# Feed-forward steps on TensorE: both high-part products in a row, then both low-part products

## The chip, the cores and the metric

The kernel runs on one core of a Trainium2 chip. The metric is the device time of one execution in microseconds (us); less is better. Its outputs are float32, and the products are made from float32 numbers split in two parts (below).

## What is computed

One layer of a small hybrid network on 256 tokens of width 1024. A mixing block (a gated linear recurrence beside an attention) is followed by a feed-forward block, and the change lies in the latter alone. Cut to that block:

```
hf = rms_norm(x, ffn_norm_g)
up = causal_depthwise_conv(hf @ w_up, ffn_conv_w, ffn_conv_b)   # w_up: 1024 x 5632, 3 taps
gate, val = split(up, 2)                                        # 2816 channels each
x = x + (gelu(gate) * val) @ w_down                             # w_down: 2816 x 1024
```

## The kernel before

**Units.** All weights come as a stream of units of 128 x 1024 float32 numbers, two to a DMA. ScalarE copies a unit to `w_hi` in the type fp32r (line L381), VectorE puts what that leaves out into `w_lo` (L703). Both tiles are rings of six buffers. The activations are split in the same way, into `h_hi` and `h_lo`, which lie side by side in `h_both`. A product is the sum of high x high, high x low and low x high.

**Steps.** The 2816 channels are 22 steps of 128 channels, numbered s = 0 to 21. A step has three units: gate, value and down. `ffn_up(s)` makes the gate's and the value's products. For each of the two, eight matmuls with 512 columns (L1419, "high" below) multiply `w_hi` with `h_hi` and `h_lo` at once, into the two halves of a bank, and then eight with 256 columns (L1423, "low") add `w_lo` times `h_hi` to the first half. The last of the low ones raises `unit_used`. `ffn_down(s)` has twelve matmuls of 512 columns (L1062, L1063, L1066), in the order high-high, low weights, low activations.

**What follows an up unit.** When `unit_used` says that a gate or value is complete, ScalarE copies the second half of its bank (`cross`, L614), and VectorE adds the first half to it (`join`, L985). ScalarE then makes the first tap of the convolution (`base`, L622), VectorE the other two (`taps`, L992 and L996), ScalarE the GELU (L628), VectorE the product with the value (`prod`, L1005), ScalarE its high part (`act_hi`, L634) and VectorE its low part (`act_lo`, L1010). Only `act_lo` raises `act_ready`, for which `ffn_down` waits.

**The order on the engines** is written out by hand, and each engine runs in order. TensorE takes `ffn_up(t)`, then `ffn_down(t - 2)`. ScalarE and VectorE, in their step t, split the weights for up(t) and down(t-2), and between these they evict what up(t-1) left:

```
# ScalarE, step t                     # VectorE, step t
hi(down_unit(t - LAG)); hi(g)         lo(down_unit(t - LAG)); lo(g)
ffn_cross(t - 1, 0)                   ffn_join(t - 1, 0)
hi(v)                                 lo(v)
ffn_cross(t - 1, 1)                   ffn_join(t - 1, 1)
ffn_base(t - 1, 0)                    ffn_taps(t - 1, 0)
ffn_act_hi(t - 2)                     ffn_act_lo(t - 2)
ffn_base(t - 1, 1)                    ffn_taps(t - 1, 1)
ffn_gelu(t - 1)                       ffn_prod(t - 1)
```

Steps 0 and 1 have code of their own on TensorE (L1372 for the high, L1383 for the low products, all of 256 columns). Steps 2 to 21 use `ffn_up`, 20 in all. The end has no up unit left to hide behind. After up(21) and down(19) TensorE goes to `ffn_end`: it waits for `act_ready` of step 20, makes three pieces of down(20), waits for `act_hi_done` of step 21, makes three pieces of down(21) (each waits for `act_ready` of step 21 before its third matmul), and then the remaining pieces of 256 columns. Beside it ScalarE and VectorE run one last step in the order above, without a gate unit: there the down unit of step 21 (`U_LAST`) stands where v stood, between the two crosses and the two joins. Up banks alternate: banks 0 and 1 in even steps, 6 and 7 in odd ones, the gate in the first of each pair.

Of the kernel before, what the change touches and what calls it, by code (L numbers as in the profile page):

```python
# [52 lines left out]
RING = 6  # L53
# [26 lines left out]
def up_units(s):  # L80
    at = U_FFN + max(3 * s - 1, 0)
    return at, at + 1
# [26 lines left out]
def build_layer(nc, x, stream, params, gates, out):  # L109
    with ExitStack() as ctx:  # L110
        def sb(name, shape, dt=F32):
            return ctx.enter_context(nc.sbuf_tensor(name, shape, dt))
# [7 lines left out]
        w_hi = [sb(f"w_hi{r}", [P, UNIT], F32R) for r in range(RING)]  # L120
        w_lo = [sb(f"w_lo{r}", [P, UNIT], F32R) for r in range(RING)]
# [120 lines left out]
        def by_chunk(tile):  # L242

            return tile[:, :].rearrange("p (kc n) -> p kc n", kc=KC)

        def up_bank(s, which):

            return bank[(0, 1, 6, 7)[2 * (s % 2) + which]]
# [21 lines left out]
        def hi_count(u):  # L270

            return u + 1 - sum(v <= u for v in VECTOR_HI)

        def lo_count(u):

            return LO_UNITS.index(u) + 1 if u in LO_UNITS else u + 1
# [24 lines left out]
        def at_pass(it, per, value):  # L301

            return value if it is None else it * per + value
# [755 lines left out]
        def _(pe):  # L1059
# [8 lines left out]
            def split(u, it=None):  # L1068

                pe.wait_ge(lo_done, at_pass(it, LOOP_UNITS, lo_count(u)))  # L1070
# [250 lines left out]
            for j in range(LC):  # L1321
                if j == LC - 1:
                    out_sums()
                u = U_O + j
# [87 lines left out]
            def ffn_up(s, it=None):  # L1412
                for which, u in enumerate(up_units(s)):
                    if s >= 2:
                        pe.wait_ge((joined_g, joined_v)[which], at_pass(it, LOOP_STEPS, s - 1))
                    whi, wlo, acc = by_chunk(w_hi[u % RING]), by_chunk(w_lo[u % RING]), up_bank(s, which)
                    pe.wait_ge(hi_done, at_pass(it, LOOP_UNITS, hi_count(u)))
                    for kc in range(KC):
                        pe.matmul(acc[:, :], whi[:, kc, :], h_both[:, kc, :, :].rearrange("p b t -> p (b t)"),  # L1419
                                  start=kc == 0, stop=False)  # L1420
                    split(u, it)
                    for kc in range(KC):
                        ins = pe.matmul(acc[:, 0:SEQ], wlo[:, kc, :], h_hi[:, kc, :], start=False, stop=kc == KC - 1)  # L1423
                    ins.then_inc(unit_used, 1)
# [34 lines left out]
            for t in range(LAG, PEELED):  # L1459
                ffn_up(t)  # L1460
                ffn_down(t - LAG)
            with pe.Fori(0, PASSES - 1) as it:
                for t in range(PEELED, PEELED + LOOP_STEPS):
                    ffn_up(t, it)
                    ffn_down(t - LAG, it)
# [64 lines left out]
```

## Time and profile before

| | |
|---|---|
| median of 3 runs | 290.15 us (289.98 to 290.15) |
| the profiled execution, its own time | 290.13 us |
| its span in the trace | 288.4 us, so 1.7 us lie outside it |
| TensorE (PE) busy | 284.1 us, 99% of the span |
| VectorE (DVE) busy | 244.2 us, 85% |
| ScalarE (ACT) busy | 202.9 us, 70% |
| feed-forward steps in `ffn_up` | 20, from about 113.8 us on |

The end of a matmul is modelled in the trace, and matmuls are pipelined, so busy shares of TensorE say little. What counts is how far apart they start, or the pieces of the chain of work that ended last, which run from one end to the next. A "weight load" (PEld) is the instruction ahead of each matmul that brings its stationary operand.

### The profile page before, as it was taken

How to read it: one execution, taken by the hardware profiler on the slowest of the kernel's cores; microseconds unless marked ns; L12 is line 12 of the kernel's file. 1: busy time of each engine (PE TensorE's matmuls, PEld its weight loads, DVE VectorE, ACT ScalarE, POOL GpSimd, SP SyncE). 2: the span in 40 equal slices, each digit the busy share in tenths (PEclk: the TensorE clock that was granted, in tenths of full speed). 3: DMA queues.
4: the chain of work that ended last, by engine and by line, in shares of the span. 5: the costliest groups of instructions: out<-in, count | busy, mean ns of one | idle time of the engine just before them, and what ended most of it. 6: DMA issues, size and time to landing. Idle time of an engine off the chain costs nothing.

```text
span 288.4 us, 5012 instructions
## 1 busy us (share of the span) xinstructions
PE 284.1 (99%) x1642; PEld 246.6 (86%) x1642; DVE 244.2 (85%) x448; ACT 202.9 (70%) x389; POOL 11.4 (4%) x26
## 2 busy tenths in 40 slices
PE   8999999999999999999999999999999999999996
PEld 7688999898788999888888888888888888888885
DVE  2998898889999888999988788888888888888765
ACT  4893599999897687778676766667666666676540
POOL 3000004600000000000000000000000000000000
PEclk9999999999999999999999999999999999999999
DMA  7999950440365705375647474544647454100003
GB/s 276 428 419 419 398 186 7 148 145 14 134 228 209 257 38 164 130 291 166 278 145 287 148 261 177 160 162 152 252 145 291 145 181 178 77 0 0 0 0 145
DMA packets 8111, 52.23 MB, mean 181 GB/s; under 512 B 928, under 2 KB 1312, under 8 KB 2080
## 3 DMA queue, kind: packets, MB, share of 16 engines
q1 hardware_dynamic: 7920, 51.50, 48.1%
q0 software_dynamic: 176, 0.53, 0.5%
q8 instruction: 9, 0.15, 0.2%
q14 instruction: 6, 0.05, 0.0%
HBM read 50.98 MB, written 1.05 MB: 180 GB/s over the span
## 4 chain that ended last, share of the span: by engine, by line
PE 95%; DMA 2%; DVE 1%; ACT 1%; SPq 0%; issue 0%
PE bank L1419 25%; PE bank L1062 15%; PE bank L1063 14%; PE bank L1066 14%; PE bank L1423 13%; PE bank L1118 3%; PE bank L1372 3%; DMA x_tok<-in_x_dram 2%; PE bank L1383 1%; PE bank L1182 1%; PE bank L1306 1%; PE bank L1213 1%; PE bank L1222 1%; PE bank L1339 1%; PE bank L1176 1%; DVE w_hi L691 0%
## 5 line engine op out<-in xcount | busy, mean ns | idle before, releaser
L703 DVE TENSOR_TENSOR w_lo<-raw,w_hi 128x1024 fp32r<-128x1024 f32 x93 | 110.9, 1221 | 4.5 <-ACT w_hi L381 3.9
L381 ACT ACTIVATE w_hi<-raw 128x1024 fp32r<-128x1024 f32 x83 | 84.2, 1058 | 2.3 <-PE bank L1066 1.9
L1419 PE MATMUL bank<-h_both,w_hi 128*128 128x512 f32 x320 | 79.6, 391 | 0.0
L1419 PEld LDWEIGHTS bank<-h_both,w_hi 128*128 128x128 f32 x320 | 58.8, 188 | 11.3
L1423 PEld LDWEIGHTS bank<-h_both,w_lo 128*128 128x128 f32 x320 | 43.7, 191 | 3.1
L1423 PE MATMUL bank<-h_both,w_lo 128*128 128x256 f32 x320 | 44.7, 283 | 0.0
L614 ACT ACTIVATE tanh_a<-bank 128x256 f32<-128x256 f32 x44 | 16.7, 381 | 38.7 <-PE bank L1423 38.7
L1063 PE MATMUL bank<-w_lo,act_hi 128*128 128x512 f32 (+1 forms) x90 | 34.9, 388 | 0.0
L1062 PE MATMUL bank<-w_hi,act_hi 128*128 128x512 f32 (+1 forms) x90 | 34.9, 388 | 0.0
L1066 PE MATMUL bank<-w_hi,act_lo 128*128 128x512 f32 (+1 forms) x90 | 34.6, 385 | 0.0
L622 ACT ACTIVATE xc<-ygate,par 128x256 f32<-128x256 f32 x44 | 26.2, 596 | 4.2 <-DVE ygate L985 4.2
L985 DVE TENSOR_TENSOR ygate<-bank,tanh_a 128x256 f32<-128x256 f32 x44 | 18.6, 422 | 12.1 <-ACT tanh_a L614 12.0
L996 DVE SCALAR_TENSOR_TENSOR xc<-ygate,par,xc 128x254 f32<-128x254 f32 x44 | 21.3, 483 | 5.1 <-DVE xc L992 0.2
L992 DVE SCALAR_TENSOR_TENSOR xc<-ygate,par,xc 128x255 f32<-128x255 f32 x44 | 21.2, 481 | 3.2 <-ACT xc L622 3.2
L1066 PEld LDWEIGHTS bank<-w_hi,act_lo 128*128 128x128 f32 x90 | 16.9, 188 | 3.5
L1062 PEld LDWEIGHTS bank<-w_hi,act_hi 128*128 128x128 f32 x90 | 17.0, 189 | 2.9
L1063 PEld LDWEIGHTS bank<-w_lo,act_hi 128*128 128x128 f32 x90 | 17.0, 189 | 2.6
L1062 PE MATMUL bank<-h_both,w_hi 128*128 128x256 f32 x64 | 18.6, 291 | 0.0
L1063 PE MATMUL bank<-h_both,w_hi 128*128 128x256 f32 x64 | 18.1, 283 | 0.0
L1066 PE MATMUL bank<-h_both,w_lo 128*128 128x256 f32 x64 | 18.1, 283 | 0.0
L628 ACT ACTIVATE gate_r<-xc 128x256 f32<-128x256 f32 x22 | 9.2, 418 | 11.1 <-DVE xc L996 11.1
L1062 PE MATMUL bank<-w_hi,mix_hi 128*128 128x512 f32 (+1 forms) x36 | 13.5, 374 | 0.0
(193 smaller groups left out, 411.4 us busy)
## 6 DMA issues: line engine op xcount, KB each, us to landing
raw<-in_stream_dram SPq DMA_DIRECT2D x47, 1024.0 KB, 4.8
x_tok<-in_x_dram SPq DMA_DIRECT2D x2, 512.0 KB, 5.0
out_dram<-x_tok SPq DMA_DIRECT2D x3, 256.0 KB, 2.1
p_T<-in_gates_dram POOLq DMA_DIRECT2D x1, 512.0 KB, 9.5
out_dram<-x_tok SPq DMA_DIRECT2D x2, 128.0 KB, 2.0
par<-in_params_dram SPq DMA_DIRECT2D x1, 117.0 KB, 6.6
mix_g<-in_params_dram POOLq DMA_DIRECT2D x1, 4.0 KB, 5.6
```

What stands on the lines that cost most here:

```text
L381: act.activation(hi_tile(u)[:, :], raw_unit(u), ACT.Copy).then_inc(hi_done, 1)
L614: act.activation(cross[which][s % 2], up_bank(s, which)[:, SEQ:2 * SEQ], ACT.Copy).then_inc(cross_out, 1)
L622: act.activation((conv_g, conv_v)[which][s % 2], joined[which][s % 2], ACT.Identity, bias=par[:, bass.ds(col + FFN_B, 1)], scale=par[:, ba ...
L703: dve.tensor_tensor(w_lo[u % RING][:, :], raw_unit(u), hi_tile(u)[:, :].bitcast(F32), ALU.subtract).then_inc(lo_done, 1)
L985: dve.tensor_tensor(joined[which][s % 2], up_bank(s, which)[:, 0:SEQ], cross[which][s % 2], ALU.add).then_inc((joined_g, joined_v)[which], 1)
L992: dve.scalar_tensor_tensor(acc[:, 1:SEQ], joined[which][s % 2][:, 0:SEQ - 1], par[:, bass.ds(col + (FFN_W + 2 * STEPS), 1)], acc[:, 1:SEQ] ...
L996: dve.scalar_tensor_tensor(acc[:, 2:SEQ], joined[which][s % 2][:, 0:SEQ - 2], par[:, bass.ds(col + FFN_W, 1)], acc[:, 2:SEQ], ALU.mult, AL ...
L1062: pe.matmul(acc, lhs_hi, rhs_hi, start=first, stop=False, skip_group_check=resumed)
L1063: pe.matmul(acc, lhs_hi, rhs_lo, start=False, stop=False, skip_group_check=resumed)
L1066: return pe.matmul(acc, lhs_lo, rhs_hi, start=False, stop=last, skip_group_check=resumed)
L1419: pe.matmul(acc[:, :], whi[:, kc, :], h_both[:, kc, :, :].rearrange("p b t -> p (b t)"), start=kc == 0, stop=False)
L1423: ins = pe.matmul(acc[:, 0:SEQ], wlo[:, kc, :], h_hi[:, kc, :], start=False, stop=kc == KC - 1)
```

## The change

In `ffn_up` the loop over gate and value is cut in two. The first loop makes the high products of the gate and then those of the value; the second makes the low products of the gate and then those of the value. The down unit follows as before. The number of matmuls, their shapes and their operands stay, and so do the waits, each of which goes with the products that it guards. The other engines' programs are the same.

```diff
                 for which, u in enumerate(up_units(s)):
                     if s >= 2:
                         pe.wait_ge((joined_g, joined_v)[which], at_pass(it, LOOP_STEPS, s - 1))
-                    whi, wlo, acc = by_chunk(w_hi[u % RING]), by_chunk(w_lo[u % RING]), up_bank(s, which)
+                    whi, acc = by_chunk(w_hi[u % RING]), up_bank(s, which)
                     pe.wait_ge(hi_done, at_pass(it, LOOP_UNITS, hi_count(u)))
                     for kc in range(KC):
                         pe.matmul(acc[:, :], whi[:, kc, :], h_both[:, kc, :, :].rearrange("p b t -> p (b t)"),
                                   start=kc == 0, stop=False)
+                for which, u in enumerate(up_units(s)):
+                    wlo, acc = by_chunk(w_lo[u % RING]), up_bank(s, which)
                     split(u, it)
                     for kc in range(KC):
                         ins = pe.matmul(acc[:, 0:SEQ], wlo[:, kc, :], h_hi[:, kc, :], start=False, stop=kc == KC - 1)
                     ins.then_inc(unit_used, 1)
```

TensorE's rows in the last step of the loop's body, before the change, with the semaphores that a row waits for; bank6 is the gate's and bank7 the value's:

```order
L1066 MATMUL bank3<-w_hi2,act_lo 128x512
L1415 REGISTER_ALU
L1419 MATMUL bank6<-h_both,w_hi0 128x512 [waits hi_done,joined_g]
L1419 MATMUL bank6<-h_both,w_hi0 128x512 x7
L1070 REGISTER_ALU
L1423 MATMUL bank6<-h_both,w_lo0 128x256 [waits lo_done]
L1423 MATMUL bank6<-h_both,w_lo0 128x256 x7
L1419 MATMUL bank7<-h_both,w_hi1 128x512 [waits hi_done,joined_v]
L1419 MATMUL bank7<-h_both,w_hi1 128x512 x7
L1070 REGISTER_ALU
L1423 MATMUL bank7<-h_both,w_lo1 128x256 [waits lo_done]
L1423 MATMUL bank7<-h_both,w_lo1 128x256 x7
```

The same place in the changed kernel:

```order
L1419 MATMUL bank6<-h_both,w_hi0 128x512 [waits hi_done,joined_g]
L1419 MATMUL bank6<-h_both,w_hi0 128x512 x7
L1419 MATMUL bank7<-h_both,w_hi1 128x512 [waits hi_done,joined_v]
L1419 MATMUL bank7<-h_both,w_hi1 128x512 x7
L1070 REGISTER_ALU
L1425 MATMUL bank6<-h_both,w_lo0 128x256 [waits lo_done]
L1425 MATMUL bank6<-h_both,w_lo0 128x256 x7
L1070 REGISTER_ALU
L1425 MATMUL bank7<-h_both,w_lo1 128x256 [waits lo_done]
L1425 MATMUL bank7<-h_both,w_lo1 128x256 x7
L1070 REGISTER_ALU
L1062 MATMUL bank4<-w_hi5,act_hi 128x512 [waits act_ready,lo_done]
```

The gate's low products have moved behind the value's high ones, so that wide matmuls stand next to wide ones and narrow next to narrow, and the gate (bank6) is complete eight wide matmuls later than before, while the value (bank7) keeps its place in the count.

After the last step the rows of TensorE are the same in both kernels; these are the first of `ffn_end` (bank4 holds a piece of the output):

```order
L1062 MATMUL bank4<-w_hi2,act_hi 128x512 [waits act_ready,lo_done]
L1063 MATMUL bank4<-w_lo2,act_hi 128x512
L1066 MATMUL bank4<-w_hi2,act_lo 128x512
```

## Rows read from the trace of the kernel before

**Rows 1.** The page: busy time, and the chain that ended last by engine.
```profile
PE 284.1 (99%) x1642; PEld 246.6 (86%) x1642; DVE 244.2 (85%) x448; ACT 202.9 (70%) x389; POOL 11.4 (4%) x26
...
PE 95%; DMA 2%; DVE 1%; ACT 1%; SPq 0%; issue 0%
```

**Rows 2.** Busy time by stretch, of one step: PE, PEld, DVE, ACT, POOL, clock.
```profile
180.26:188.57 8.31, 8.31 (x46) 7.17 (x44) 6.92 (x12) 5.50 (x10) 0.00 (x0) 1.00 0.54 170
```

**Rows 3.** The chain in order of time: start us, us, what; steps 10 and 21.
```profile
180.43 1.81 PE bank L1419 x8
182.24 0.95 PE bank L1423 x8
183.19 1.84 PE bank L1419 x8
185.03 0.95 PE bank L1423 x8
...
271.80 1.81 PE bank L1419 x8
```

**Rows 4.** The chain in order of time, steps 0 to 2.
```profile
108.19 1.92 PE bank L1383 x16
...
113.94 1.84 PE bank L1419 x8
```

**Rows 5.** Timeline, steps 2 and 3: start us, us, engine, line, instruction.
```profile
118.53 0.42 DVE L1010 TENSOR_TENSOR act_lo<-gate_i,act_hi 128x256 fp32r<-128x256 f32 x1
119.37 0.40 PE L1062 MATMUL bank<-w_hi,act_hi 128*128 128x512 f32 x1
121.13 1.05 ACT L381 ACTIVATE w_hi<-raw 128x1024 fp32r<-128x1024 f32 x1
122.11 0.62 PE L1419 MATMUL bank<-h_both,w_hi 128*128 128x512 f32 x2
122.91 1.22 DVE L703 TENSOR_TENSOR w_lo<-raw,w_hi 128x1024 fp32r<-128x1024 f32 x1
124.05 0.42 DVE L985 TENSOR_TENSOR ygate<-bank,tanh_a 128x256 f32<-128x256 f32 x1
124.38 0.48 DVE L992 SCALAR_TENSOR_TENSOR xc<-ygate,par,xc 128x255 f32<-128x255 f32 x1
```

**Rows 6.** Timeline, step 21 and the end.
```profile
274.60 0.38 ACT L614 ACTIVATE tanh_a<-bank 128x256 f32<-128x256 f32 x1 [1.65 <-PE bank L1423]
274.88 1.05 ACT L381 ACTIVATE w_hi<-raw 128x1024 fp32r<-128x1024 f32 x1
...
275.97 1.22 DVE L703 TENSOR_TENSOR w_lo<-raw,w_hi 128x1024 fp32r<-128x1024 f32 x1 [0.52 <-ACT w_hi L381]
...
277.81 0.42 DVE L985 TENSOR_TENSOR ygate<-bank,tanh_a 128x256 f32<-128x256 f32 x1 [0.62 <-ACT tanh_a L614]
...
278.30 0.48 DVE L992 SCALAR_TENSOR_TENSOR xc<-ygate,par,xc 128x255 f32<-128x255 f32 x1
...
279.22 0.42 DVE L1010 TENSOR_TENSOR act_lo<-gate_i,act_hi 128x256 fp32r<-128x256 f32 x1
...
279.76 0.19 PEld L1062 LDWEIGHTS bank<-w_hi,act_hi 128*128 128x128 f32 x1
279.95 0.39 PE L1062 MATMUL bank<-w_hi,act_hi 128*128 128x512 f32 x1
...
281.12 0.42 ACT L634 ACTIVATE act_hi<-gate_i 128x256 fp32r<-128x256 f32 x1 [1.36 <-DVE gate_i L1005]
...
281.57 0.43 DVE L1010 TENSOR_TENSOR act_lo<-gate_i,act_hi 128x256 fp32r<-128x256 f32 x1 [0.49 <-ACT act_hi L634]
...
282.46 0.39 PE L1066 MATMUL bank<-w_hi,act_lo 128*128 128x512 f32 x1
```

**Rows 7.** Timeline, where TensorE had waited for VectorE.
```profile
12.09 0.18 PEld L1118 LDWEIGHTS bank<-w_hi,h_both 128*128 128x128 f32 x1 [0.32 <-DVE w_hi L691]
12.12 0.47 PE L1118 MATMUL bank<-w_hi,h_both 128*128 128x512 f32 x1
```

## The prediction, made before the changed kernel ran

> **What bounds the kernel now.** I read the page first. TensorE is busy for 99% of the span, and of the chain that ended last 95% is TensorE [rows 1]. The reader should not stop at the busy share, since ends of matmuls are modelled; so the second view is one step of the feed-forward block by stretch. It takes 8.31 us, TensorE fills it at the full granted clock (1.00, that is 2.4 GHz), VectorE is busy for 6.92 us of it and ScalarE for 5.50 [rows 2]. The third view is the chain in order of time. From step 10 to step 21 the gate's high products begin at 180.43 and 271.80 [rows 3]: 11 steps in 91.37 us, 8.31 each, without a piece of another engine between. In the steady steps nothing is waited for on TensorE, so only its own spacing can give time back there. The last view is the timeline of the end, where up products no longer cover what follows them: there the other engines can take time away.
>
> **Part 1: spacing on TensorE, 20 steps.** Inside a step the two groups of eight high matmuls do the same work, yet the gate's takes 1.81 us and the value's 1.84 [rows 3]. The gate's follows a down unit (512 columns), the value's follows low products (256 columns). So a group of wide matmuls behind narrow ones costs 0.03 us more. It does not grow with the number of narrow ones ahead: the first high group of step 2 comes behind 5.75 us of 256-column matmuls (108.19 to 113.94, some 48 at 0.12 each) and takes 1.84 as well [rows 4]. In the changed kernel the value's high group follows the gate's high group, so I give it 1.81: 0.03 us less a step. The down unit still follows narrow products and pays as before. Against this, eight low ones behind wide ones take 0.95 us [rows 3], and 16 in a row 1.92, so 0.96 for a second eight [rows 4]; the 16 low ones of a step will take 0.95 + 0.96 instead of 2 x 0.95, 0.01 more. Net 0.02 us a step, and over 20 steps 0.4 us saved. Its bounds: 0 if the 0.03 us belong to something else than the neighbour, 20 x 0.03 = 0.6 if the second low group costs nothing more.
>
> **Part 2: the waits in the steady steps.** The value's high products now start where the gate's low ones did, 0.95 us sooner, and need `hi(v)` and the join of two steps ago by then. Step 3 is the tightest. Its first high matmul starts at 122.11, so the value's will start at 122.11 + 1.81 = 123.92; `hi(v)` runs there from 121.13 and ends at 122.18 [rows 5]. Spare 1.7 us. The join in question is that of step 1, before the stretch of these rows. The gate's `lo` is needed 1.81 us later than before, the value's at the same time. The down unit starts at the same place: in step 2 `act_lo` ends at 118.53 + 0.42 = 118.95, and the down unit's first matmul is at 119.37 [rows 5]; in that step what leads to `act_lo` hangs on steps 0 and 1, which don't change.
>
> The gate itself is complete 1.81 us later in its step. ScalarE's `cross` for the gate waits for that, and behind it in ScalarE's order stand `hi(v)`, the value's cross, the bases and `act_hi`; behind VectorE's join of the gate stand `lo(v)`, the value's join, the taps, `act_lo`, `prod`, and the weight splits of the next step. So VectorE's round moves back against TensorE's. How far is worked out in part 3 (0.96 us). It moves once and not each step as long as a round fits into a step: VectorE has 8.31 - 6.92 = 1.39 us idle in a step [rows 2], and the idle time that the change puts between the gate's join and `lo(v)` is `hi(v)` 0.28 after the cross, `lo(v)` 1.09 after `hi(v)`, less the join at 0.42 after the cross and its 0.33: 0.62 us [rows 5, 6]. This fits. Everything that VectorE makes in a round is used by TensorE in the next one, so I cost this shift at nothing while there is a next round. Cover gone, the price is that of the next part. DMAs are issued by a queue that waits for `lo`; they move by the same 0.6 to 1 us against buffers that come round only every four steps.
>
> **Part 3: the end.** After up(21) and down(19) TensorE needs `act_lo` of step 20 at once. VectorE makes it in its last round, behind the gate's join of step 21. Before, that was on time with nothing over: `act_lo` ends at 279.22 + 0.42 = 279.64, the weight load that waits for it starts at 279.76, and the matmul at 279.95 [rows 6]. Now the same chain in the changed kernel, with the steps before 21 held at their old times:
> - TensorE's chain of step 21 begins at 271.80 [rows 3]. Gate complete at 271.80 + 1.81 + 1.81 + 0.95 = 276.37 (before: 271.80 + 1.81 + 0.95 = 274.56, with the cross at 274.60, 0.04 later [rows 3, 6]). Cross of the gate 276.41.
> - `hi(U_LAST)` 0.28 later, 276.69; `lo(U_LAST)` 1.09 after that, 277.78 (274.60, 274.88, 275.97 [rows 6]).
> - Join of the value: VectorE is now busy with `lo` until then, and a join behind a `lo` starts 1.14 after it (122.91, 124.05 [rows 5]), 278.92. It was 277.81.
> - Taps of the gate 0.33 later (124.05, 124.38 [rows 5]), 279.25. They were at 278.30, 0.49 behind the join [rows 6]. So the shift is 0.95 to 0.96.
> - `act_lo(20)` stands 0.92 behind the first tap, 280.18, and ends at 280.60. The weight load follows 0.12 after (279.64 to 279.76), 280.72.
> - The first matmul after a wait: where TensorE had waited for VectorE, the weight load starts at 12.09 and the matmul ends at 12.12 + 0.47 = 12.59, as one of 0.39 would that started at 12.20, so 0.11 behind its load [rows 7]. That gives 280.83.
> - Without the wait it would start at 279.95 - 0.02 = 279.93. The stall is 0.90 us.
>
> Bounds of the stall: 0.72 to 1.0 us. The lower one lets the matmul hide all of the 0.19 between load and matmul, the upper one keeps 0.96 whole, with the load's restart on top. After the stall nothing else is late. `act_hi(21)` will end at 281.12 + 0.42 + 0.96 = 282.50, so its matmul could start at 282.50 + 0.12 + 0.11 = 282.73, and TensorE gets to it at 282.46 - 0.45 + 0.88 = 282.89. `act_lo(21)` will end at 281.57 + 0.43 + 0.96 = 282.96, its matmul could start at 283.19, and TensorE comes at 282.46 + 0.88 = 283.34 [rows 6]. Behind it the final adds and stores follow TensorE as before.
>
> **Sum.** -0.4 (20 x 0.02) + 0.9 = +0.5 us. The profiled execution took 290.13 us, so 290.6; it lies 0.02 under the median of 290.15, so the same number holds for the median. About 0.2% of the time, 0.58 us, is what a measurement of this kernel can tell from no change: slower begins at 290.73, faster at 289.57. I expect a small loss just inside that.
>
> **Rivals.**
> *The order is free on TensorE, and only the end pays (slower).* Then the saving of part 1 is absent and the stall stays: 290.15 + 0.9 = 291.05. For it speaks that 0.03 us a group is small and its cause is not visible in the trace; against it that all value groups in the part of the chain that I read show it and no gate group behind a down unit does. It decides from a saving under 0.3 us. The Trainium skill has a rule of this kind: "TensorE: Matmul & The Clock Gate", section on the back-to-back issue gap, gives an isolated gap of N/2.4 + 2.5 ns at full clock, a function of the matmul's own columns. By that rule a reordering saves nothing. The rows speak against its use here, since 512 columns take 1.81 or 1.84 us for eight depending on what is ahead, and 256 columns some 0.12 us each where half of 1.81/8 is 0.113 [rows 3]; the same section says that the spacing is set by load and matmul together, which fits them better.
>
> *VectorE's round no longer fits (slower).* If the late gate made a round longer than 8.3 us, the lag would grow from step to step, and TensorE would wait in each step once it had used up its lead. It starts when the idle time added in a round passes 1.39 us against my 0.62. At an overrun of 0.1 us, over the 18 steps less the lead, it costs up to 1.8 us: 292 or so with the end. Against it stands the margin of 0.8 us.
>
> *The end is covered after all.* If `act_lo(20)` were not late, for instance since VectorE's joins did not wait as I think, only the saving is left: 290.15 - 0.4 = 289.75, no change by the measure. Against it: in the old trace there are only 0.12 us from the end of `act_lo(20)` to the load that needs it [rows 6].
>
> *Wide next to wide gives more (faster).* If the value group lost its extra and the down unit also lost part of it, 2 x 0.03 a step, 1.2 us, with a stall at its lower bound, it would be 289.65; to pass 289.57 the end must be covered too. I see nothing for it but the unknown cause of the 0.03 us.
>
> **Chances.** My forecast with its own small errors 0.67, of which 0.13 lies over 290.73 (a stall nearer to 1.0, or a saving nearer to 0.3) and the rest within; order free 0.12; round too long 0.06; end covered 0.09, within; more given back 0.06, most of it faster. So faster 0.06, within 0.63, slower 0.31. The likeliest case alone spans 290.3 to 290.9. The range for eight times in ten reaches up to the first rival, and down to an end that is half covered (a stall of 0.4 to 0.5 less the saving): 290.0 to 291.1. Outside lie the covered end, most of what gives more, and the round that is too long.
>
> **What would show it.** In the chain of the changed kernel: value high groups of 1.81 us like the gate's, a piece of 16 low matmuls of 1.91, and a step of 8.29 us (if 8.31, part 1 is wrong). In the timeline: gate crosses directly behind 16 wide and 8 narrow matmuls, no idle time of TensorE from step 2 to down(19), and VectorE's taps some 0.95 us later against TensorE. At the end one gap of TensorE of about 0.7 us ahead of the first L1062 of down(20), put down to `act_lo` on VectorE, and none ahead of down(21). The prediction is wrong if the gap is missing, if a second one opens at `act_hi` of step 21 (0.16 us spare), or if TensorE waits in any steady step.

## The result

The changed kernel takes 290.56 us (median of 22 runs, 290.28 to 290.80), the kernel before 290.07 us (22 runs, 289.94 to 290.20). The ratio is 1.0017, with a 95% interval of 1.0011 to 1.0023: 0.49 us slower, inside the 0.2% that the prediction took for no change, though the interval leaves out 1. It forecast 290.6 us and plus 0.5.

### The profile after

The page of the changed kernel, its busy times and its chain by engine. Beside [rows 1], TensorE is at 98% instead of 99%, and 93% of the chain instead of 95%; VectorE has gained a share of the chain:

```profile
PE 283.9 (98%) x1642; PEld 246.5 (85%) x1642; DVE 242.6 (84%) x448; ACT 201.0 (70%) x389; POOL 11.4 (4%) x26
...
PE 93%; DMA 2%; DVE 2%; ACT 1%; issue 0%; SPq 0%
```

The chain of the changed kernel in order of time (start us, us, what), for steps 2, 10 and 21 and the end:

```profile
113.98 3.65 PE bank L1419 x16
117.63 1.91 PE bank L1425 x16
...
180.30 3.63 PE bank L1419 x16
183.93 1.91 PE bank L1425 x16
...
271.45 3.63 PE bank L1419 x16
275.08 0.97 PE bank L1425 x8
276.09 0.26 issue
276.35 1.06 ACT w_hi L381
277.43 1.23 DVE w_lo L703
278.66 0.34 DVE ygate L985
279.00 0.40 DVE xc L992
279.42 0.48 DVE xc L996
279.90 0.35 DVE act_lo L1010
280.25 0.14 issue
280.39 0.46 PE bank L1062
```

Two things are to be seen. The 16 high products take 3.63 us, where [rows 3] have 1.81 + 1.84 = 3.65, and the 16 low ones 1.91, where they have 2 x 0.95 = 1.90. In step 2 the high ones take 3.65, since the first group there follows narrow ones as in [rows 4]. From step 10 to step 21 there are 91.15 us, so 8.29 a step instead of 8.31. And at the end the chain leaves TensorE in the middle of step 21's low products, when the gate is complete, and comes back to it at the first matmul of down(20). In between lie the copy of the last down unit, its subtraction, the value's join, the gate's taps and `act_lo`, the links that the prediction named.

The same links in the timeline of the changed kernel:

```profile
276.07 0.38 ACT L614 ACTIVATE tanh_a<-bank 128x256 f32<-128x256 f32 x1 [2.94 <-PE bank L1425]
276.35 1.05 ACT L381 ACTIVATE w_hi<-raw 128x1024 fp32r<-128x1024 f32 x1
...
277.43 1.23 DVE L703 TENSOR_TENSOR w_lo<-raw,w_hi 128x1024 fp32r<-128x1024 f32 x1 [0.52 <-ACT w_hi L381]
...
278.58 0.42 DVE L985 TENSOR_TENSOR ygate<-bank,tanh_a 128x256 f32<-128x256 f32 x1
...
278.91 0.47 DVE L992 SCALAR_TENSOR_TENSOR xc<-ygate,par,xc 128x255 f32<-128x255 f32 x1
...
279.82 0.42 DVE L1010 TENSOR_TENSOR act_lo<-gate_i,act_hi 128x256 fp32r<-128x256 f32 x1
...
280.39 0.46 PE L1062 MATMUL bank<-w_hi,act_hi 128*128 128x512 f32 x1 [0.65 <-DVE act_lo L1010]
```

In [rows 6] no wait of TensorE stands ahead of down(20). Here it waits 0.65 us by the record; since ends of matmuls are modelled, the loss is larger, 0.88, worked out below. `act_lo` ends at 280.24.

### The profile page after: what moved, and what is told of

Its sections match the earlier page's. It is cut to its first block, busy times and chain, and to the rows that moved or that the text cites. A ratio compares the mean times of both kernels' runs of the same rounds, so it can differ in the third digit from the quotient of the medians.

```text
span 288.9 us, 5012 instructions
## 1 busy us (share of the span) xinstructions
PE 283.9 (98%) x1642; PEld 246.5 (85%) x1642; DVE 242.6 (84%) x448; ACT 201.0 (70%) x389; POOL 11.4 (4%) x26
## 4 chain that ended last, share of the span: by engine, by line
PE 93%; DMA 2%; DVE 2%; ACT 1%; issue 0%; SPq 0%
PE bank L1419 25%; PE bank L1062 14%; PE bank L1063 14%; PE bank L1066 14%; PE bank L1425 13%; PE bank L1118 3%; PE bank L1372 3%; DMA x_tok<-in_x_dram 2%; PE bank L1383 1%; PE bank L1182 1%; PE bank L1306 1%; PE bank L1213 1%; PE bank L1222 1%; PE bank L1339 1%; PE bank L1176 1%; DVE w_hi L691 0%
## 5 line engine op out<-in xcount | busy, mean ns | idle before, releaser
L1419 PE MATMUL bank<-h_both,w_hi 128*128 128x512 f32 x320 | 75.8, 389 | 0.0
L1419 PEld LDWEIGHTS bank<-h_both,w_hi 128*128 128x128 f32 x320 | 60.0, 188 | 12.4
L1425 PEld LDWEIGHTS bank<-h_both,w_lo 128*128 128x128 f32 x320 | 41.0, 191 | 1.6
L1425 PE MATMUL bank<-h_both,w_lo 128*128 128x256 f32 x320 | 41.5, 283 | 0.0
L1066 PE MATMUL bank<-h_both,w_lo 128*128 128x256 f32 x64 | 18.1, 283 | 0.0
```

Source lines behind the costliest of these rows:

```text
L1066: return pe.matmul(acc, lhs_lo, rhs_hi, start=False, stop=last, skip_group_check=resumed)
```

## The experiments

Each run was timed beside the kernel before, and its ratio stands with it. That kernel's median was 290.08 us beside the first three runs below and the turns of one and one, and 290.07 beside the others. A line `...` in a cut of code or of a view stands for lines left out.

### Step 21 alone in the old order

```diff
-            with pe.Fori(0, PASSES - 1) as it:
+            with pe.Fori(0, PASSES - 2) as it:
                 for t in range(PEELED, PEELED + LOOP_STEPS):
                     ffn_up(t, it)
                     ffn_down(t - LAG, it)
+            for t in range(STEPS - LOOP_STEPS, STEPS):
+                (ffn_up_old if t == STEPS - 1 else ffn_up)(t)
+                ffn_down(t - LAG)
```

`ffn_up_old`, whose text is left out, is `ffn_up` of the kernel before.

> The changed kernel, with the last pass of TensorE's loop written out and step 21 alone in the old order (gate high, gate low, value high, value low). The theory: the saving comes from the wide groups that stand next to each other in steps 2 to 20 (19 x 0.02 = 0.38 us) and the stall at the end comes from the late gate of step 21 alone. Then the gap ahead of down(20) is gone and the time is 290.07 - 0.38 = 289.7, up to 0.1 more for the pass written out. First rival: VectorE's whole round is late against TensorE since the loop began, and step 21's own order does not bring it back; then a gap of 0.4 us or more stays, 290.1 to 290.6. Second rival: the order is free on TensorE, no saving; then 290.07 without a gap.

Measured: 289.62 us, ratio 0.9984 (0.9975 to 0.9993). The chain of this run shows step 21 with its old pieces, and no piece of another engine follows until the final adds:

```profile
271.22 1.81 PE bank L1435 x8
273.03 0.95 PE bank L1439 x8
273.98 1.84 PE bank L1435 x8
275.82 0.95 PE bank L1439 x8
```

The stall is gone and the saving is there (290.08 - 0.38 = 289.70 was expected). That VectorE's round was late in all steps before did no harm: it catches up in the one step in which the gate is early again. The timeline of this run has the `act_lo` of step 20 at

```profile
278.64 0.42 DVE L1010 TENSOR_TENSOR act_lo<-gate_i,act_hi 128x256 fp32r<-128x256 f32 x1
```

It ends 279.06 - 271.22 = 7.84 us behind the start of step 21, as in the kernel before (279.64 - 271.80 [rows 3, 6]); in the changed kernel it is 280.24 - 271.45 = 8.79. The first rival, a gap of 0.4 us or more that stays, falls. The second falls too: with the order free there would be no gain.

### Step 21 alone in the new order

```diff
-            with pe.Fori(0, PASSES - 1) as it:
+            with pe.Fori(0, PASSES - 2) as it:
                 for t in range(PEELED, PEELED + LOOP_STEPS):
                     ffn_up(t, it)
                     ffn_down(t - LAG, it)
+            for t in range(STEPS - LOOP_STEPS, STEPS):
+                (ffn_up_new if t == STEPS - 1 else ffn_up)(t)
+                ffn_down(t - LAG)
```

`ffn_up_new`, left out too, is `ffn_up` of the changed kernel.

> The kernel before, with the last pass of TensorE's loop written out and step 21 alone in the new order. The theory: the whole loss at the end, 0.88 us of stall ahead of down(20), less 0.02 of saving, so 290.07 + 0.87 = 290.9, and up to 0.1 more for the pass written out. First rival, the stall needs VectorE's round to be late since the loop began: less than half of it, 290.1 to 290.5. Second rival, order free: 290.07 + 0.89 = 291.0, not to be told from the theory by the time; the value's high group of step 21 tells (1.81 against 1.84 us).

Measured: 290.97 us, ratio 1.0030 (1.0019 to 1.0042), so plus 0.89. One step in the new order carries the whole loss. The waits of this run, from 270 us on, have the same entry as the changed kernel:

```profile
PE bank L1062 <- DVE act_lo L1010: 0.6, 1, 0.6
```

The high products of step 21 take 3.63 us for 16, the gain of that one step, while the steps before keep their 1.81 and 1.84.

### The last down unit split ahead of the gate's eviction

```diff
             hi(down_unit(STEPS - 2))
-            ffn_cross(STEPS - 1, 0)
             hi(U_LAST)
+            ffn_cross(STEPS - 1, 0)
...
             lo(down_unit(STEPS - 2))
-            ffn_join(STEPS - 1, 0)
             lo(U_LAST)
+            ffn_join(STEPS - 1, 0)
```

> The changed kernel, with two moves at the end and none in the steps: ScalarE makes the high part of the last down unit before it waits for step 21's gate, and VectorE its low part before the gate's join. The theory says that what makes the last act_lo of step 20 late is not the late gate as such but the copy and the subtraction of the last down unit that are queued behind its eviction (hi 0.28 behind the cross, lo 1.09 behind that, join 1.14 behind that). With them ahead, the taps of the gate come 0.9 us sooner, the gap ahead of down(20) is gone, and 290.56 - 0.88 = 289.7. Rival: the chain from the gate's eviction is late by itself (it is complete 1.8 us later); then 0.3 us or more of the gap stay, 290.0 to 290.6.

Measured: 289.63 us, ratio 0.9986 (0.9976 to 0.9995). All 20 steps are in the new order here, and the stall is gone. In the timeline of this run the gate's cross is as late as in the changed kernel, behind 2 us of idle time of ScalarE, but both splits are done by then, and `act_lo` comes at 278.74 in place of 279.82:

```profile
271.97 2.00 ACT L381 ACTIVATE w_hi<-raw 128x1024 fp32r<-128x1024 f32 x2
273.42 2.35 DVE L703 TENSOR_TENSOR w_lo<-raw,w_hi 128x1024 fp32r<-128x1024 f32 x2
...
275.96 0.38 ACT L614 ACTIVATE tanh_a<-bank 128x256 f32<-128x256 f32 x1 [1.99 <-PE bank L1425]
...
278.74 0.42 DVE L1010 TENSOR_TENSOR act_lo<-gate_i,act_hi 128x256 fp32r<-128x256 f32 x1
279.46 0.40 PE L1062 MATMUL bank<-w_hi,act_hi 128*128 128x512 f32 x1
```

So the late gate by itself costs nothing even at the end. What costs is the work that stood behind its eviction in the order of two engines.

### The same two moves in the kernel before

> The kernel before, with the two moves of the run that put the last down unit's split ahead of step 21's gate eviction, and nothing else. The theory: in the kernel before VectorE's last act_lo of step 20 was on time, so there is nothing to win, 290.07 (289.9 to 290.2), and the 0.93 us that the same moves gave in the changed kernel were the price of its late gate. Rival: the moves shorten the end by themselves; then the time falls by 0.2 us or more here too.

Measured: 290.10 us, ratio 0.9999 (0.9990 to 1.0008). The moves give nothing without the change, and 290.56 - 289.63 = 0.93 us with it. They take back a price of the change and are no gain of their own.

### High and low products in turns

Three runs of the kernel before, with an up unit's products mixed in steps 6 to 21. In the first, high and low ones take turns one by one; the other two make two and four high ones, then as many low ones. The wait for the low part (`split`) stands ahead of all of them now, but the lists of waits of the three runs have none of TensorE from step 2 on. The edit of the first is shown as a change of `ffn_up`; it stands in a copy of it, which the loop over steps 6 to 21 calls:

```diff
+                    split(u, it)
                     for kc in range(KC):
                         pe.matmul(acc[:, :], whi[:, kc, :], h_both[:, kc, :, :].rearrange("p b t -> p (b t)"),
                                   start=kc == 0, stop=False)
-                    split(u, it)
-                    for kc in range(KC):
                         ins = pe.matmul(acc[:, 0:SEQ], wlo[:, kc, :], h_hi[:, kc, :], start=False, stop=kc == KC - 1)
```

> The kernel before, with the products of an up unit in steps 6 to 21 in turns: one high (512 columns), one low (256 columns), eight times. It tells what the 0.03 us of a wide group behind narrow ones is. If each wide matmul that follows a narrow one pays a fixed price like the group's 0.03 us, there are 14 more such places a step: 16 x 14 x 0.03 = 6.3 us more, 296. If narrow matmuls in a row run up a debt in weight loads (0.120 us each where half a wide one is 0.113) that the next wide ones pay off, a single narrow one runs up none: 16 x 0.006 + 2 x 0.028 = 0.14 us less a step, 16 steps, 287.9. If the first wide one behind a narrow one pays its first 7 ns each time (0.234 for 0.227) and the narrow one gains its 6 ns, nothing changes, 290.

> As the run with one high and one low product in turns, steps 6 to 21 of the kernel before, now two high and two low in turns. One narrow matmul ahead cost the wide ones behind it 9 ns (step 8.387 against 8.307 us), eight cost 28 ns. If the price grows with the narrow ones in a row up to that limit, two cost some 18: a step gets 8 x 18 + 8 x 234 + 16 x 226.6 = 5.64 us of up products against 5.56, plus 0.08 x 16 = 1.3 us, 291.4. If it is at the limit of 28 ns from two on, 0.16 x 16 = 2.6 us, 292.7. If a border costs 9 ns whatever is ahead of it, nothing changes or the time falls: 290.0.

> The same with four high and four low in turns. If the price of a border is at its limit of 28 ns by four narrow matmuls: 4 x 28 + 4 x 474 + 16 x 226.6 = 5.63 us against 5.56, 0.07 x 16 = 1.2 us more, 291.3. If it grows in proportion up to eight (14 ns at four): 5.58, 290.4.

| in turns | time | ratio (95%) |
|---|---|---|
| one and one | 291.39 us | 1.0044 (1.0030 to 1.0057) |
| two and two | 289.85 us | 0.9992 (0.9983 to 1.0001) |
| four and four | 290.84 us | 1.0025 (1.0015 to 1.0035) |

None of the three mechanisms written ahead of the first run holds: it lost 1.31 us, between "nothing" and 6.3. From it I took 9 ns for a single narrow matmul ahead of a wide one, and the expected 291.4 for pairs missed as well; pairs are not slower than the kernel before at all. The case with the same 9 ns at every border (290.0) came nearest to them, but it has no room for the fours, which have half as many borders and take 1.0 us more than the pairs. Fours came between their two forecasts.

The chains of the three runs, one in each fence. One and one:

```profile
180.67 0.23 PE bank L1434
180.90 0.12 PE bank L1436
...
186.31 0.23 PE bank L1062
...
272.93 0.23 PE bank L1434
```

Two and two:

```profile
180.32 0.45 PE bank L1435 x2
180.77 0.23 PE bank L1438 x2
...
185.88 0.23 PE bank L1062
...
188.61 0.45 PE bank L1435 x2
...
271.54 0.45 PE bank L1435 x2
```

Four and four:

```profile
180.55 0.91 PE bank L1435 x4
181.45 0.47 PE bank L1438 x4
181.93 0.93 PE bank L1435 x4
...
272.43 0.91 PE bank L1435 x4
```

The up products of a step last 186.31 - 180.67 = 5.64 us in ones; in the kernel before they last 185.03 + 0.95 - 180.43 = 5.55 [rows 3]. The 11 steps from 10 to 21 take 272.93 - 180.67 = 92.26 us in ones, 271.54 - 180.32 = 91.22 in twos and 272.43 - 180.55 = 91.88 in fours, against 91.37: 8.39, 8.29 and 8.35 us a step against 8.31. Carried over to 16 steps that makes plus 1.29, minus 0.22 and plus 0.74 us, where the times show plus 1.31, minus 0.22 and plus 0.77. The gain of the pairs lies within the interval of their times, but all their steps in the trace have it. It doesn't lie in the up products, which last 185.88 - 180.32 = 5.56 us, but in the down unit behind them: 188.61 - 185.88 = 2.73 us, against 8.31 - 5.55 = 2.76 in the kernel before. So the neighbours do set the spacing, by up to 0.1 us a step. The price of a border is not a function of the narrow matmuls ahead that I could name.

### The low products behind the down unit

```diff
+            def down_before_low(t, it=None):
+                ffn_up(t, it, low=False)
+                ffn_down(t - LAG, it)
+                ffn_low(t, it)
...
             with pe.Fori(0, PASSES - 2) as it:
                 for t in range(PEELED, PEELED + LOOP_STEPS):
-                    ffn_up(t, it)
-                    ffn_down(t - LAG, it)
+                    down_before_low(t, it)
```

Steps 4, 5 and 18 to 20 are written in the same way outside the loop, and step 21 is in the old order. The table of the order in which units are used (`CONSUMED`) follows. `ffn_up` with `low=False` makes the high products alone, `ffn_low` the low ones.

> The changed kernel with step 21 in the old order (as in the first run), and in steps 4 to 20 the low products moved behind the down unit too: gate high, value high, down, gate low, value low. Gate and value are complete another 2.7 us later in their step. The number of borders between narrow and wide stays. The theory says that a later completion costs nothing while there is a next step: act_lo of step t-2 ends 3.43 us into step t by the changed kernel's round, and the down unit's first matmul stands at 3.63 with its load 0.2 ahead: just in time, stall 0 to 0.1 a step, so 289.6 to 291.3, with the lower end likelier; if it fits, the time is that of the first run. Rival: VectorE's or ScalarE's round, with the gate so late, no longer fits, TensorE waits 0.3 us or more in each of 16 steps: over 294.

Measured: 292.45 us, ratio 1.0080 (1.0067 to 1.0094). That lies above the whole range of the theory, 289.6 to 291.3, and under the rival's 294: both missed. The round of VectorE fits, its result is just not in time. The chain of this run in one step:

```profile
180.75 3.65 PE bank L1419 x16
184.41 0.32 PE bank L1062
...
187.24 1.91 PE bank L1429 x16
189.15 2.07 PE bank L1419 x9
```

Its timeline at the place where the down unit waits:

```profile
183.69 0.42 DVE L1010 TENSOR_TENSOR act_lo<-gate_i,act_hi 128x256 fp32r<-128x256 f32 x1
184.22 0.19 PEld L1062 LDWEIGHTS bank<-w_hi,act_hi 128*128 128x128 f32 x1 [0.24 <-issue]
...
188.23 0.38 ACT L614 ACTIVATE tanh_a<-bank 128x256 f32<-128x256 f32 x1 [2.10 <-PE bank L1429]
```

`act_lo` ends at 184.11, the weight load starts 0.11 later, and the first matmul takes 0.32 of the chain instead of 0.23. A step is 189.15 - 180.75 = 8.40 us, 0.11 more than in the changed kernel: 0.09 of it is this wait, and 0.02 comes from the high products, which now follow narrow ones in each step and take 3.65 us instead of 3.63. ScalarE still stands idle for 2.10 us until the gate is complete, so the other engines' round is not too long. The wait comes back all the same, since the gate's low products now stand behind the down unit: by what TensorE waits, the next gate is complete later, and with it the next `act_lo`.

How little was missing can be worked out from the changed kernel. There `act_lo` ends 4.93 us before the down unit's first matmul (the rows are in the next section). Here the gate is complete about 2.75 us later in its step, and the down unit begins 1.91 us sooner, as the low products no longer stand ahead of it. That leaves 0.27 us, and from the end of `act_lo` to where the first matmul begins to count this run needs 184.41 + 0.32 - 0.23 - 184.11 = 0.39. The expectation had left no time for this restart.

From step 3 to step 21 the longer steps make 1.73 of the 2.83 us by which this run is above the first one, its twin: in the two timelines the first high matmuls of these steps start at 122.10 and 272.99 here, 150.89 us apart, and at 121.89 and 271.05 there, 149.16 apart. The rest is a stall at the end, ahead of down(20):

```profile
272.99 2.00 PE L1439 MATMUL bank<-h_both,w_hi 128*128 128x512 f32 x8
...
282.39 0.47 PE L1062 MATMUL bank<-w_hi,act_hi 128*128 128x512 f32 x1 [0.91 <-DVE act_lo L1010]
```

From the start of step 21 to the end of that matmul there are 282.39 + 0.47 - 272.99 = 9.87 us; in the first run there are 279.37 + 0.39 - 271.05 = 8.71, so 1.16 less. The round is too late to catch up in one step, and this part the expectation had not counted at all.

## Why the prediction was right

**Spacing, 0.4 us saved.** Right in kind and size. From step 2 to step 21 TensorE's chain moved from 271.80 - 113.94 = 157.86 us to 271.45 - 113.98 = 157.47, so 0.39 less over 19 steps. With the 0.02 of step 21 itself that is 0.41. It comes from the 1.84 us groups, which are gone from every step but the first (3.65 there). The first run isolates it: minus 0.46 us without the stall. How the 0.02 us of a step divides into 0.03 gained and 0.01 lost is at the last digit of the chain and not shown; the sum over 19 steps is. In the last run, where the 16 high products follow narrow ones again, they take 3.65 us again.

**The waits in the steady steps, nothing.** Right. The round did move against TensorE, and the changed kernel's list of waits has none of TensorE from step 2 to down(19). The `act_lo` of step 8, in the timelines of the changed kernel and of the kernel before:

```profile
180.49 0.42 DVE L1010 TENSOR_TENSOR act_lo<-gate_i,act_hi 128x256 fp32r<-128x256 f32 x1
```

```profile
179.82 0.42 DVE L1010 TENSOR_TENSOR act_lo<-gate_i,act_hi 128x256 fp32r<-128x256 f32 x1
```

The down unit of step 10 needs it, and begins at 183.93 + 1.91 = 185.84 and at 185.03 + 0.95 = 185.98 [rows 3]. So there are 4.93 us to spare where there were 5.74, 0.8 less; 0.96 had been forecast. The prediction called the shift free without working out this spare time in a steady step; it was ample. The first run shows that one early gate brings the round back, and the last run how far the lateness can be carried.

**The end, 0.90 us lost.** Right, link by link: cross, hi, lo, join, taps and `act_lo` of step 20 were forecast, with the steps before held, at 276.41, 276.69, 277.78, 278.92, 279.25 and 280.18. They came at 276.07, 276.35, 277.43, 278.58, 278.91 and 279.82, all 0.34 to 0.36 sooner, which is the saving that the forecast had held out (271.80 against 271.45 for the start of the step). From the start of step 21 to the end of the first matmul of down(20) there are 280.39 + 0.46 - 271.45 = 9.40 us; before, there were 279.95 + 0.39 - 271.80 = 8.54 [rows 3, 6]. That is 0.86 more, with the 0.02 that the step saves in it, so the stall is 0.88. The second run measures this alone: plus 0.89, with 0.02 of saving in it. No second gap opened at `act_hi` of step 21.

**Sum.** -0.41 + 0.88 = +0.47, and +0.49 was measured. In the one profiled execution of each kernel the start of step 2 is 0.04 later as well (113.94 to 113.98), nothing that the change touches.

**The rivals.** The order free on TensorE (and with it the rule of the Trainium skill, "TensorE: Matmul & The Clock Gate", back-to-back issue gap, by which the gap is a function of the matmul's own columns) would have given 291.05. The measured time and the other orders speak against it. What a rule on the matmul's own columns leaves out here is the difference between the orders, 0.01 to 0.1 us in a step of 8.3. VectorE's round too long: not seen. The end covered after all: not so by itself, but the two moves cover it. Wide next to wide gives more: not seen either, what is left of a step for the down unit is 8.29 - 3.63 - 1.91 = 2.75 us, against 2.76 before.

**What stays open** is the mechanism behind the dear neighbours. Run length 1, 2, 4, 8 and 16 of each kind give up-and-down steps of 8.39, 8.29, 8.35, 8.31 and 8.29 us. That is no monotone price. The single gaps between starts of matmuls, read from the trace of the kernel before as means over steps 7 to 19, show where it is paid: behind eight narrow matmuls the first five wide ones take 234, 236, 228, 232 and 231 ns until the next starts, and the later ones 227. That is 28 ns, spread over five matmuls. So the length of the wide run matters too, which the forecasts for the turns had left out. In the run of the pairs the down unit, behind two narrow ones, takes 233 and 231 ns and then 227, 10 ns in all. I did not find what sets this, and the forecast worked since it took its 0.03 us from the same neighbours that it was about.

**A version that beats both.** Both ways of taking the stall away, step 21 in the old order or the last down unit split first, give 289.62 and 289.63 us: 0.15% under the kernel before. The second moves one line in each of two programs and writes no code out.

## What to carry to other kernels

When an engine is full, its order of work still moves two things, its own spacing (here 0.02 us a step) and the moment at which a result is complete for others. In the middle of a pipelined loop the second is free up to the spare time that the result has before it is needed. Work that out, with the restart after a wait in it: 0.8 of 5.7 us cost nothing here, and an order that left 0.27 us made TensorE wait in every step. Look at the last pass by itself: there the cover is gone, and what costs is often not the late result but unrelated work queued behind its eviction; move that work ahead of the wait.

## What the runs showed of the hardware that I had not expected

With weights loaded for each matmul, wide (512 columns) and narrow (256) matmuls in turns of one cost 0.08 us a step more than in groups of eight (8.39 against 8.31), turns of four 0.05 more (8.35), and turns of two 0.01 less (8.29). So a count of the borders between wide and narrow does not give the time: the run with the most borders loses, the one with half as many gains a little, and the one with a quarter loses again. The extra time of wide matmuls behind eight narrow ones is spread over the first five of them (28 ns in all), not paid by the first alone.
